# Layer norms of a two-block transformer kernel: the first application step of the second half of the features moves from VectorE to GpSimd

## The reference

```python
def layer_norm(x, g, b):
    mu = mean(x); xc = x - mu
    return xc * rsqrt(mean(xc * xc) + 1e-5) * g + b

def post_norm(x, delta, g, b):
    return layer_norm(ALPHA * x + delta, g, b)

for i in range(2):
    x = post_norm(x, 0.5 * swiglu(x), ...)
    x = post_norm(x, mixer(x), ...)          # forgetting attention, then latent attention
    x = post_norm(x, 0.5 * swiglu(x), ...)
    x = post_norm(x, sigmoid(x @ w + c) * (p @ w_proj), ...)
```

## Time and profile before

| what | value |
| --- | --- |
| median of 3 runs | 1952.99 us |
| profiled execution | 1951.09 us |
| its span, first to last instruction | 1949.8 us |
| PE busy | 1794.7 us (92%) |
| DVE busy | 1089.2 us (56%) |
| ACT busy | 886.7 us (45%) |
| POOL busy | 103.3 us (5%) |
| mean granted TensorE clock | 0.957 |

### The profile page before, as it was taken

The page is one execution under the profiler, slowest core; times in us unless marked ns, Lnnn a source line. Parts: engine busy times, 40 slices in busy tenths (PEclk is TensorE's granted clock), DMA queues, the critical chain, the costliest instruction groups (busy, mean ns, idle before and its releaser), DMA issues.

```text
span 1949.8 us, 27887 instructions
## 1 busy us (share of the span) xinstructions
PE 1794.7 (92%) x11764; PEld 1610.8 (83%) x11764; DVE 1089.2 (56%) x1696; ACT 886.7 (45%) x1515; POOL 103.3 (5%) x116
## 2 busy tenths in 40 slices
PE   7999897898999999989998999779998998899985
PEld 7999877676999899978868999669997776799974
DVE  5545556994545555554756545465455555555455
ACT  4444553443544444445645444444443554344443
POOL 0000001221000000001210000100000000100000
PEclk9999998989999999999988999889998999899997
DMA  8455350005555455435334455344544222464521
GB/s 336 173 189 184 109 175 33 1 1 227 198 191 189 142 209 193 172 122 195 131 130 186 178 193 177 147 155 173 187 173 157 82 98 83 160 226 174 184 108 43
DMA packets 31964, 301.38 MB, mean 155 GB/s; under 512 B 3792, under 2 KB 4320, under 8 KB 5984
## 3 DMA queue, kind: packets, MB, share of 16 engines
q1 hardware_dynamic: 31840, 299.60, 42.0%
HBM read 298.52 MB, written 1.06 MB: 154 GB/s over the span
## 4 chain that ended last, share of the span: by engine, by line
PE 80%; DVE 12%; ACT 5%; issue 2%; POOL 1%; DMA 0%; SPq 0%; DVEq 0%; ACTq 0%
PE bank L351 43%; PE bank L360 29%; DVE w_lo L323 2%; ACT w_hi L316 2%; DVE x L575 1%; PE bank L375 1%; PE bank L389 1%; DVE x L599 1%; DVE w_raw L1119 1%; PE bank L390 1%; POOL rstd L657 1%; DVE w_raw L1189 1%; PE bank L1298 1%; DVE w_raw L1138 1%; ACT w_raw L961 1%
## 5 line engine op out<-in xcount | busy, mean ns | idle before, releaser
L323 DVE TENSOR_TENSOR w_lo<-w_raw,w_hi 128x1024 fp32r<-128x1024 f32 (+4 forms) x545 | 609.8, 1171 | 387.0 <-ACT w_hi L316 386.2
L351 PE MATMUL bank<-xT_hi,w_hi 128*128 128x256 f32 x2264 | 642.3, 284 | 4.7 <-DVE w_lo L323 4.1
L316 ACT ACTIVATE w_hi<-w_raw 128x1024 fp32r<-128x1024 f32 (+4 forms) x561 | 524.5, 995 | 264.7 <-PE bank L360 264.7
L351 PE MATMUL bank<-xT_hi,w_lo 128*128 128x256 f32 x2264 | 639.7, 283 | 0.0
L351 PE MATMUL bank<-xT_lo,w_hi 128*128 128x256 f32 x2264 | 639.7, 283 | 0.0
L351 PEld LDWEIGHTS bank<-xT_hi,w_hi 128*128 128x128 f32 x2264 | 432.8, 191 | 16.2 <-DVE w_lo L323 5.4
L351 PEld LDWEIGHTS bank<-xT_lo,w_hi 128*128 128x128 f32 x2264 | 433.0, 191 | 5.7
L351 PEld LDWEIGHTS bank<-xT_hi,w_lo 128*128 128x128 f32 x2264 | 433.2, 191 | 0.0
L360 PE MATMUL bank<-w_hi,hT_lo 128*128 128x512 f32 x528 | 208.6, 395 | 0.0
L360 PE MATMUL bank<-w_lo,hT_hi 128*128 128x512 f32 x528 | 208.6, 395 | 0.0
L360 PE MATMUL bank<-w_hi,hT_hi 128*128 128x512 f32 x528 | 208.4, 395 | 0.0
(11 more groups left out here) (296 smaller groups left out, 2071.2 us busy)
## 6 DMA issues: line engine op xcount, KB each, us to landing
w_raw<-in_ffn_a SPq DMA_DIRECT2D x22, 1536.0 KB, 6.7
w_raw<-in_ffn_b SPq DMA_DIRECT2D x22, 1536.0 KB, 6.6
w_raw<-in_ffn_c SPq DMA_DIRECT2D x22, 1536.0 KB, 6.6
w_raw<-in_ffn_d SPq DMA_DIRECT2D x22, 1536.0 KB, 6.5
w_raw<-in_ffn_e SPq DMA_DIRECT2D x22, 1536.0 KB, 6.6
w_raw<-in_ffn_f SPq DMA_DIRECT2D x22, 1536.0 KB, 6.6
gains<-in_gains SPq DMA_DIRECT2D x11, 1024.0 KB, 4.9
w_raw<-in_mla_up SPq DMA_DIRECT2D x8, 1280.0 KB, 5.6
```

Of the source, the lines that this page charges most:

```text
L316: nc.scalar.activation(w_hi[c.pair][:, a:b], raw[c.slot][:, a:b], ACTF.Copy).then_inc(w_hi_made, 1)
L323: nc.vector.tensor_tensor(w_lo[c.pair][:, a:b], raw[c.slot][:, a:b], w_hi[c.pair][:, a:b].bitcast(F32), ALU.subtract).then_inc(w_lo_made, 1)
L351: ins = nc.tensor.matmul(o, w[:, c], a[:, k, :], start=(n == 0), stop=(n == last))
```

## The change

In norms 4 to 10, for the two pieces of the second half of the features, the first application step is no longer one DVE instruction. It is made by POOL in two instructions of 128x512: an add of minus the mean, repeated along the row, and a multiplication by the gain. POOL issues them for block `b` right behind the root of block `b`. DVE waits for the new semaphore `centred` in place of its own first step. The first half of the features, and norm 11 (whose slice starts at 0), stay as they were.

```diff
-        minus_half_made, mean_made = sem("minus_half_made"), sem("mean_made")
+        minus_half_made, mean_made, centred = sem("minus_half_made"), sem("mean_made"), sem("centred")
...
             dve.wait_ge(squared, 2 * n + b + 1)
-            m = dve_own.step(nc.vector.scalar_tensor_tensor(xb, xb, minus_mean[:, b:b + 1], gains[:, c], ALU.add, ALU.mult))
+            if c.start:
+                dve.wait_ge(centred, 4 * (n - 4) + 2 * b + 2)
+            else:
+                m = dve_own.step(nc.vector.scalar_tensor_tensor(xb, xb, minus_mean[:, b:b + 1], gains[:, c], ALU.add, ALU.mult))
+                dve_own.wait(m)
             dve.wait_ge(rooted, 2 * n + b + 1)
-            dve_own.wait(m)
             nc.vector.scalar_tensor_tensor(xb, xb, rstd[:, b:b + 1], gains[:, D + c.start:D + c.stop],
                                            ALU.mult, ALU.add).then_inc(normed, 1)
...
                 nc.gpsimd.tensor_tensor(rstd[:, b:b + 1], rstd[:, b:b + 1], expo[:, 0:1], ALU.pow).then_inc(rooted, 1)
+                if 4 <= n < N_TURNED:
+                    pool_centre(n, b)
+
+        def pool_centre(n, b):
+
+            xb = x[:, b, half_of(1)]
+            pool.wait_ge(gains_landed, 16 * (n + 1))
+            pool.wait_ge(mean_made, 2 * (n - 4) + b + 1)
+            pool.wait_ge(squared, 2 * n + b + 1)
+            nc.gpsimd.tensor_tensor(xb, xb, minus_mean[:, b:b + 1].to_broadcast([P, D // 2]), ALU.add).then_inc(centred, 1)
+            pool.wait_ge(centred, 4 * (n - 4) + 2 * b + 1)
+            nc.gpsimd.tensor_tensor(xb, xb, gains[:, half_of(1)], ALU.mult).then_inc(centred, 1)
```

## The result

Over 20 runs the changed kernel takes 1957.26 us in the median (1952.61 to 1959.77); over the same number the kernel before takes 1951.2 us (1944.73 to 1955.9). The ratio is 1.0034, 95% interval 1.0024 to 1.0043: 6.6 us slower, between 4.7 and 8.4. The forecast was 8.9 us. One execution of a later experiment ran in a slower state (2532 us at a mean granted clock of 0.646, against 0.951 to 0.961 in all others) and is in no ratio here.

A forecast was written before the change was run, and what follows sets the result against it. PE, busy 92%, was taken to pay for each norm's length. Norms 4, 5, 7, 9 gave +9.0, norm 8 +1.7, norm 6 -0.35, norm 10 -1.45: +8.9 us, 1960.0, put on the median as 1961.9; range 1955 to 1968.

The forecast's parts named there:

- The step that waits: Second application step (L599), for which PE's transposes idle 43.8 us in 20 waits; first products follow piece 2 by 0.83.
- The sign named for this: Prediction is wrong if PE's wait for L599 grows by less than 6 us in norms 4, 5, 7 and 9 together.
- The prices: POOL add 1.04 us, multiplication 1.25 alone or 1.13 behind DVE's end; DVE's L599 ends 0.60 behind POOL.
- Who goes first: Behind a root DVE waits for, POOL's next instruction goes before DVE's: add 0 before L599 of piece 0.
- Rival A: DVE goes first at L599 of piece 0: piece 2 +1.3 us, +3.9 in all, 1955.0 us; chance 0.11.
- The chain of one norm: POOL and DVE holding each other from root 0: root 1 at 3.86, piece 2 +2.25 us, piece 3 +1.68.
- Norms 6, 8 and 10: Norm 8 follows piece 3, +1.7 us; in norms 6 and 10 piece 3 leaves sooner, -0.35 and -1.45.
- Rival B: Only POOL's queue counts, engines don't hold each other for 128x512: -2.9 us, 1948.2 us; chance 0.08.
- Rival C: POOL's add and multiplication take 0.48 us each, over before block 1's variance: -8.7 us, 1942.4 us; chance 0.05.
- Rival D: Slower side: 0.1 us per handover between POOL's instructions, adding 1.4 us, and TensorE's clock low for longer; chance 0.08.

The follow-up runs named there:

- a later experiment: The change in norms 4, 5, 7 and 9 alone, against the kernel before: ratio 1.0039 (1.0024 to 1.0055), +7.6 us.
- the run with fills: The kernel before, with three POOL fills of an unused tile behind each root of norms 4 to 10, DVE unchanged: ratio 1.0011, +2.1 us.
- the unused tile: The kernel before, with POOL making the change's add and multiplication on a 128x512 tile DVE never touches, DVE keeping its first steps: ratio 1.0074, +14.4 us.
- the one with the early steps: The kernel before, with DVE making the first steps of pieces 2 and 3 early in norms 6 and 10, nothing on POOL: 1943.97 us, ratio 0.9964.

## Why the prediction was right, and where it was off

*The step that waits.* Right. PE idles for piece 2 in norms 4, 5, 7 and 9, and its first products are 0.82 us behind it, as before. The sign named for this, 6 us or more of added wait in these four norms, came at 8.2.

*The prices.* The add: forecast 1.04, measured 1.03 to 1.04 in 14 of 14. The multiplication: 1.13 behind DVE's end, measured 1.13. DVE behind POOL: 0.60, measured 0.55 (871.72 to 872.27). The groups (their shortest, median, longest ns):

```profile
L670 POOL TENSOR_TENSOR x<-x,minus_mean x14: 1033/1035/1040, 870.7 to 1903.7; 128x512 f32<-128x512 f32 x14
```

```profile
L672 POOL TENSOR_TENSOR x<-x,gains x14: 1593/1600/1623, 871.8 to 1904.8; 128x512 f32<-128x512 f32 x14
```

*Who goes first.* POOL, in all 14 places, as L1148 had it. Rival A falls by the trace. It gave +1.3 for piece 2 because it assumed DVE first in each contest; where DVE was made to go first in front of the adds, the first step of piece 1 was held instead and norms 4, 5, 7, 8 and 9 still cost +1.8 or more each.

*The chain of one norm.* Forecast and measured in norm 4, behind root 0: piece 0 1.60 and 1.56; root 1 3.86 and 3.77; piece 1 5.46 and 5.33; piece 2 7.19 and 7.01; piece 3 8.67 and 8.52. Each of the steps up to piece 2 was put 0.04 to 0.05 too long, mostly DVE's restart behind POOL, and they add up: +2.25 was forecast for the first products and +2.06 measured. Over four norms this is 0.8 us.

*Norms 6, 8 and 10.* +1.7 forecast and +1.51 measured in 8; -0.35 and -0.69 in 6; -1.45 and -1.75 in 10. The signs are right, but the size in norm 6 is within what that norm differs by without the change (0.73 in the run with fills). 1.6 us of the forecast's sum are these sizes: 8.9 against 7.3 counted in the trace.

*Rival B* falls by L602 at 1.44 us and by the fills. *Rival C* falls by the prices: the add took 1.03 us and the multiplication ended 1.13 us behind DVE, not 0.48 each. *Rival D* falls by the add's 1.03 us. For handing work over between POOL's own instructions it took 0.1 us, which no row gave, and it added 1.4 us where 14 times 2 of these would be 2.8; the gap was 0.08 us between add and multiplication on the unused tile and 0.05 to 0.06 between the fills.

Rival D also said that TensorE's clock would stay low for longer because PE idles longer. PE did idle longer, and the clock did not stay low for longer. By the granted clock in slices of 0.25 us from a stage's first matmul on, it was at its lower level for 4.7, 5.2, 5.1, 2.7, 5.3, 3.1 and 6.1 us in norms 4 to 10 before, and for 2.6, 2.5, 3.9, 3.5, 5.7, 3.0 and 4.4 us after. Norm 5 in the kernel before and in the changed one (window; its length, PE busy, matmuls; mean granted clock; DMA share; GB/s):

```profile
1031.00:1043.00 12.00, 12.00 (x77) 0.75 0.45 166
```

```profile
1031.00:1043.00 12.00, 11.22 (x81) 0.85 0.50 168
```

The changed kernel starts its products at 1032.25, 0.53 us later than the other, and has the higher clock, 0.85 against 0.75. Across nine profiled executions (all but the 2532 us one) these stretches run from 2.0 to 6.2 us, and not by the idle time before them: norm 4 has 4.7 us in the kernel before and 2.0 us in the one with the early steps, which is the same up to there. So the traces don't show that longer idle time costs clock, and one trace of each kernel is too few to rule it out.

*Why the two profiles differ by 2.2 us only.* Root 0 of norm 4 ends 2.2 us earlier in the changed kernel, in code that is the same. The seven norms cost +7.3. From first products to the next root 0 the seven stages take 3.1 us less, 1011.0 to 1007.9; the stretches at the lower clock are 6.6 us shorter in sum, and as matmuls of 256 columns start 0.213 us apart at the lower level and 0.12 at the higher, 44% of that, 2.9 us, is what the lower level costs. Norm 11 takes 0.16 more by the order of the waits. -2.2 + 7.3 - 3.1 + 0.2 = +2.2. The prediction set itself against one profiled execution and moved it by the 1.9 us to the median of three runs; over 20 runs the median of before was 1951.2, so of the 4.6 us by which the forecast of 1961.9 was high, 1.8 are that footing and 2.8 the size of the change (8.9 against 6.1 between the medians). 1.6 of these 2.8 are counted in the trace; the rest stays open within the interval.

*What was missed.* The prediction has no term for the swap of the two waits. In the changed kernel it is hidden in norms 4 to 10, because the piece is held by the add anyway.

## What to carry to other kernels

An engine that is busy 5% of the time is not a free hand. Look at what stands behind the new work in its queue (here a one-element root on which all depended), and at whether the two engines can read at the same time. Price the exclusion from any place in the trace where the two met before, and remember that it hits one-element instructions too. Before moving work to another engine, look for a gap of the same engine: the two first steps cost nothing where DVE had been waiting for PE.

## What the runs showed of the hardware

- DVE with two SBUF operands and POOL reading SBUF exclude each other for the whole instruction (L602 1.44 us instead of 0.75, L565 1.05 instead of 0.16, and POOL's multiplication 1.60, ending 1.13 us behind DVE); POOL's fills don't take part (DVE 0.75 us beside a 0.95 us fill), nor do DVE instructions with an operand in PSUM (L611 0.68 us beside L672). This is what the Trainium skill (SBUF — State Buffer, "Who interferes with whom") states, and the runs agree.
- An instruction that had waited ended earlier behind its release than its duration alone: a root at 0.40 instead of 0.55, an L602 at 0.55 instead of 0.75. So part of an instruction seems to be done while it waits; the runs don't show which part.
- The order of two waits on DVE cost 0.08 us: DVE sat idle for 0.44 us in front of its second step when the wait for the root came first, and for 0.52 us when it came last.
